# Long convolution: each way-back bank is scaled and emptied by ScalarE into one of four places, with VectorE mixing from there; in the odd layer, both tiles' means stand ahead of one weight quarter

## The chip, the cores and the metric

The kernel runs on one core of a Trainium2 chip. The metric is the device time of one execution in microseconds (us), the median of the runs. Its engines are TensorE (PE, with PEld for its weight loads), VectorE (DVE), ScalarE (ACT), GpSimd (POOL) and SyncE (SP, which issues the weight DMAs). Each engine works through its own instructions in order and waits on semaphores where another engine must have finished first.

## The reference

A latent sequence of 256 tokens and a context of 256 tokens, 1024 wide, in fp32, go through an even layer (a long convolution beside attention), an odd layer (a chunkwise mLSTM), and then two layers of a second model. The two places that the change touches compute this:

```python
def bidir_long_conv(u, filt):
    n = u.shape[1]
    uf = jnp.fft.rfft(u.astype(jnp.float32), n=2 * n, axis=1)
    ff = jnp.fft.rfft(filt, axis=0)
    return jnp.fft.irfft(uf * ff[None], n=2 * n, axis=1)[:, :n].astype(u.dtype)

def hyena_mixer(xv, conv_w, conv_b, f_w1, f_b1, f_freq, f_w2, f_b2, f_w3, hy_bias):
    ...
    x0, x1, v = _split(dw_conv(xv, conv_w, conv_b), (HY_WIDTH, HY_WIDTH, HY_WIDTH))
    filt = hyena_filter(n, f_w1, f_b1, f_freq, f_w2, f_b2, f_w3)
    g = v * x1
    return x0 * (bidir_long_conv(g, filt) + g * hy_bias.astype(g.dtype))
...
        x_lat = x_lat + ga_l[:, None] * rms_norm(y_lat, g_post[layer])
```

The filter is divided by the sum of its absolute values per channel; the kernel applies that factor (`snorm`) to the convolution's result.

## The kernel before

Every fp32 product is made of three fp32r matmuls (lead x lead, lead x rest, rest x lead, line 153). The weights come as a stream: SP loads pieces of 1 MB into a ring of four; ACT rounds each quarter piece to its lead (line 307) and DVE takes the rest (line 144), three quarters ahead of PE; each of the two waits on the one before it. Layers are `Stage` objects whose per-engine programs yield a position in time; `merge` sorts the steps of one engine by that position, and this fixes each engine's order when the program is built. Nothing moves while it runs.

**The long convolution** (`LongConv`) runs between matmul groups of the projections (`dense1`): 2 sequences x 2 halves of 512 channels = 4 rounds. One round: PE transforms tokens to spectra (line 1466), in two halves h = 0 and 1, into PSUM banks 4, 6 and 5, 7 in pairs; ACT copies one bank of each pair (line 1476) and DVE forms sum and difference (lines 1487, 1488); DVE makes twelve products (line 1500) and four folds (line 1526); PE goes back to tokens in four blocks of 128 channels, ch = 0 to 3 (line 1541, 8 short matmuls in the trace). All four blocks write the same half of the same bank, `banks[2]`. After each block DVE runs three steps (`mixes`): it takes the bank times `snorm` into the one scratch `y1` (line 1554, tile `cond`), adds g x bias (line 1556) and multiplies with x0 (line 1557), which raises `lc_mixed`. PE's next block waits for `lc_mixed`, and so do both halves of the next round's spectra. Between two blocks PE has six matmuls of a projection group, in round 1 also four transposes (line 1442), and none between blocks 2 and 3 of round 3, nor between block 3 and the spectra in round 2. The projection groups of that time are the third short convolution (DVE lines 1385 and 1387 after ACT line 1867) and then the gate (ACT line 1896, Silu, and DVE line 1902, which waits for `lc_mixed` of its chunk). PE may write a group's bank again only when DVE has read the group four before it. Line 1585 rounds the sources of the output projection to their leads on ACT.

**The odd layer's seam**: the output projection ends tile 0's two groups first; twelve matmuls of tile 1 follow. `Residual` (tag `or_`) then does for each of two token tiles: ACT squares the two banks with a sum (line 1620), DVE takes the mean (line 1634), ACT the root (line 1628), DVE the reciprocal (line 1642), and DVE twice a product of 512 columns (line 1649) and an addition to x (line 1664). PE's transposes of x for the next layer (line 614, eight blocks) wait for x: the first four blocks for the third addition, the others for the fourth. ACT's leads (line 622) and DVE's rests (line 630) follow each block; blocks 4 to 7 reuse four banks and wait for the rest of the block four before. Where in the queues the steps stand is set by `places`, a row for each tile: position of the squares, of the root (the mean 0.05 ahead of it), of the products, of the additions. `at` is the end of the output projection.

Of the kernel before, what the change touches and what calls it, by code (L numbers as in the profile page):

```python
# [7 lines left out]
ALU = mybir.AluOpType  # L8
ACT = mybir.ActivationFunctionType
# [7 lines left out]
SEQ = 256  # L17
# [1373 lines left out]
class LongConv(Stage):  # L1391
# [4 lines left out]
    def __init__(self, core, room, att, dense, gT, x0T, X, gtok, Y, T2, snorm, banks, start, step):  # L1396
        self.core, self.room, self.att, self.dense, self.gT, self.x0T, self.X = core, room, att, dense, gT, x0T, X
        self.gtok, self.Y, self.T2, self.snorm, self.banks, self.start, self.step = gtok, Y, T2, snorm, banks, start, step
        s = lambda n: core.sem("lc_" + n)
        self.turned, self.tok_ready, self.tabs_turned, self.tabs_ready = s("turned"), s("tok_ready"), s("tabs_turned"), s("tabs_ready")  # L1400
        self.spect, self.copied, self.read, self.made, self.folded = s("spect"), s("copied"), s("read"), s("made"), s("folded")
        self.back, self.mixed = s("back"), s("mixed")
        self.rounds = [(s, j) for s in range(2) for j in range(2)]
        self.tensor, self.vector, self.scalar = (
            (self.tables, self.turns, self.spectra, self.inverse), (self.sums, self.products, self.folds, self.mixes), (self.tables_back, self.tokens, self.copies))

# [46 lines left out]
    def spectra(self, pe):  # L1453
        nc, ps = self.core.nc, self.core.ps
        for r, (s, j) in enumerate(self.rounds):
            for h in range(2):
# [5 lines left out]
                if r:  # L1462
                    pe.wait_ge(self.read, 2 * (r - 1) + h + 1)
                    pe.wait_ge(self.mixed, 4 * r)
                for e in range(2):
# [62 lines left out]
    def inverse(self, pe):  # L1528
        nc, ps = self.core.nc, self.core.ps
        for r, (s, j) in enumerate(self.rounds):  # L1530
            for ch in range(4):
# [5 lines left out]
                if 4 * r + ch:  # L1537
                    pe.wait_ge(self.mixed, 4 * r + ch)
                for e in range(2):
# [3 lines left out]
                mm.then_inc(self.back, 1)  # L1543

    def mixes(self, dve):
        core, nc, link = self.core, self.core.nc, self.core.dve_chain
        for r, (s, j) in enumerate(self.rounds):
            for ch in range(4):
                yield self.at(r) + 5.55 + 0.45 * ch
                k, ss = 4 * j + ch, slice(s * SEQ, (s + 1) * SEQ)  # L1550
                dve.wait_ge(self.back, 4 * r + ch + 1)
                dve.wait_ge(self.dense.dve_read, 2 * KC + k + 1)
                y = self.room.y1
                link(dve, nc.vector.tensor_scalar(y.rearrange("p (m e) -> p m e", e=2), core.ps[:, self.banks[2], 0:SEQ].rearrange("p (e m) -> p m e", e=2),
                                                  self.snorm[:, k:k + 1], None, ALU.mult))
                link(dve, nc.vector.scalar_tensor_tensor(out=y, in0=self.gT[:, k, ss], scalar=core.col("hy_bias", k), in1=y, op0=ALU.mult, op1=ALU.add))
                nc.vector.tensor_tensor(self.x0T[:, k, ss], y, self.x0T[:, k, ss], ALU.mult).then_inc(self.mixed, 1)
# [780 lines left out]
def odd_layer(core, odd):  # L2338
# [46 lines left out]
    def turn_ready(pe, n):  # L2385
        pe.wait_ge(norm.scaled, 2 * n + 2)
        if n < 4:
# [11 lines left out]
                   [core.hT[:, 2 + 2 * i:4 + 2 * i, :].rearrange("p k t -> p (k t)") for i in range(2)],  # L2399
                   [(at - 0.95, at - 0.78, at - 0.74, at - 0.73), (at + 0.01, at + 0.06, at + 0.07, at + 0.08)], parts=2)  # L2400
    end = OddEnd([gates, dense, Program(scalar=(taps,)), heads, norm, turn, out, res], (dense, out), heads, res, at)
# [890 lines left out]
```

## Time and profile before

| | us |
|---|---|
| median of 3 runs | 1885.04 (1884.64 to 1889.12) |
| profiled execution: its time | 1883.9 |
| profiled execution: span, first to last instruction | 1882.1 |
| PE busy | 1808.0 |
| DVE busy | 1141.3 |
| ACT busy | 897.6 |
| mean granted TensorE clock | 0.988 |

PE is busy for 96% of the span, so a microsecond of the kernel's time is either a matmul or one of the few gaps in which PE waits. The waits by releaser name the engine and line that ended each gap. In a timeline the bracket behind a row is the idle time just before it and what ended it; matmuls overlap, so a row's duration is longer than the distance to the next row, and ends are modelled.

### The profile page before, as it was taken

The page shows a single profiled execution, that of the slowest core. Times are in us where ns is not written, and L with a number is a line of the kernel's source. Part 1 is how long each engine was busy: PE and PEld are TensorE (multiplying, and loading weights), DVE is VectorE, ACT ScalarE, POOL GpSimd, SP SyncE. Part 2 cuts the span into 40 slices and gives each one's busy share as a digit, 9 for nine tenths or more (in the row PEclk, how much of TensorE's full clock was granted, in tenths as well). Part 3 has the DMA queues.
Part 4 walks back from the last instruction along what each step waited for, and adds up shares of the span by engine and source line. Part 5 has one row for each costly group of instructions (what it writes and reads, how often), then busy time and mean ns, then how long its engine had stood idle before and what let it go on. Part 6 is the DMA issues. An engine that isn't in the chain of part 4 may idle for free. (4 is left out here: it accounts for less than half of the span.)

```text
span 1882.1 us, 24159 instructions
## 1 busy us (share of the span) xinstructions
PE 1808.0 (96%) x9264; PEld 1474.6 (78%) x9264; DVE 1141.3 (61%) x2038; ACT 897.6 (48%) x1405; POOL 57.1 (3%) x58
## 2 busy tenths in 40 slices
PE   9999999989998999999989999999999999989998
PEld 4777788767787867777778788789987888779986
DVE  5463366687438456666766675666546656566644
ACT  3323444422226346665645556356534646536643
POOL 0000000000000000000100010000000001000000
PEclk9999999999999999999989999999999999999999
DMA  9445311211335324333345444445554444455552
GB/s 342 164 157 201 112 48 65 67 50 63 134 101 180 111 71 139 118 91 116 121 138 168 128 131 156 168 164 183 180 200 154 135 146 136 164 170 168 189 194 88
DMA packets 114843, 264.08 MB, mean 140 GB/s; under 512 B 5111, under 2 KB 9496, under 8 KB 114536
## 3 DMA queue, kind: packets, MB, share of 16 engines
q1 hardware_dynamic: 111528, 252.52, 40.9%
q0 software_dynamic: 2368, 7.70, 1.2%
q10 hardware_dynamic: 832, 2.30, 0.3%
q8 instruction: 74, 1.21, 0.3%
q14 instruction: 41, 0.34, 0.1%
HBM read 261.46 MB, written 1.05 MB: 139 GB/s over the span
## 5 line engine op out<-in xcount | busy, mean ns | idle before, releaser
L144 DVE TENSOR_TENSOR qw_rest<-weights,qw_lead 128x1024 fp32r<-128x1024 f32 (+2 forms) x428 | 522.3, 1223 | 451.8 <-ACT qw_lead L307 450.2
L307 ACT ACTIVATE qw_lead<-weights 128x1024 fp32r<-128x1024 f32 (+2 forms) x428 | 448.3, 1048 | 542.9 <-PE psum L153 529.0
L153 PE MATMUL psum<-qw_lead,b_h_lead 128*128 128x512 f32 (+1 forms) x480 | 198.8, 414 | 9.1 <-DVE hT L3004 5.4
L153 PE MATMUL psum<-qw_lead,b_h_rest 128*128 128x512 f32 (+1 forms) x480 | 188.4, 392 | 0.0
L153 PE MATMUL psum<-qw_rest,b_h_lead 128*128 128x512 f32 (+1 forms) x480 | 187.9, 392 | 0.0
L153 PE MATMUL psum<-b_h_lead,qw_lead 128*128 128x256 f32 x512 | 145.5, 284 | 0.0
L153 PE MATMUL psum<-b_h_rest,qw_lead 128*128 128x256 f32 x512 | 145.2, 284 | 0.0
L153 PE MATMUL psum<-b_h_lead,qw_rest 128*128 128x256 f32 x512 | 145.2, 284 | 0.0
L153 PE MATMUL psum<-e_h_lead,qw_lead 128*128 128x512 f32 x320 | 141.8, 443 | 1.8 <-DVE e_qT L1387 1.4
L153 PE MATMUL psum<-e_h_lead,qw_rest 128*128 128x512 f32 x320 | 126.5, 395 | 0.0
L153 PE MATMUL psum<-e_h_rest,qw_lead 128*128 128x512 f32 x320 | 125.6, 392 | 0.0
L153 PEld LDWEIGHTS psum<-qw_lead,b_h_lead 128*128 128x128 f32 x480 | 91.5, 191 | 30.5 <-DVE hT L3004 6.3
L153 PE MATMUL psum<-qw_lead,o_h_lead 128*128 128x512 f32 x256 | 107.3, 419 | 3.5 <-PEq L118 3.1
L153 PEld LDWEIGHTS psum<-qw_lead,b_h_rest 128*128 128x128 f32 x480 | 91.1, 190 | 19.0
L153 PEld LDWEIGHTS psum<-qw_rest,b_h_lead 128*128 128x128 f32 x480 | 91.6, 191 | 15.2
L153 PE MATMUL psum<-qw_lead,o_h_rest 128*128 128x512 f32 x256 | 100.9, 394 | 0.0
L153 PE MATMUL psum<-qw_rest,o_h_lead 128*128 128x512 f32 x256 | 100.6, 393 | 0.0
L153 PE MATMUL psum<-qw_rest,b_upT_lead 128*128 128x512 f32 x256 | 99.8, 390 | 0.0
L153 PE MATMUL psum<-qw_lead,b_upT_lead 128*128 128x512 f32 x256 | 99.8, 390 | 0.0
L153 PE MATMUL psum<-qw_lead,b_upT_rest 128*128 128x512 f32 x256 | 99.7, 390 | 0.0
L153 PEld LDWEIGHTS psum<-b_h_lead,qw_lead 128*128 128x128 f32 x512 | 98.4, 192 | 0.3
L153 PEld LDWEIGHTS psum<-b_h_rest,qw_lead 128*128 128x128 f32 x512 | 98.4, 192 | 0.0
(480 smaller groups left out, 3482.9 us busy)
## 6 DMA issues: line engine op xcount, KB each, us to landing
weights<-in_w_in SPq DMA_DIRECT2D x48, 1024.0 KB, 5.1
weights<-in_o_w_in SPq DMA_DIRECT2D x32, 1024.0 KB, 5.4
weights<-in_w_mlp_up SPq DMA_DIRECT2D x32, 1024.0 KB, 5.5
weights<-in_w_mlp_down SPq DMA_DIRECT2D x32, 1024.0 KB, 4.8
weights<-in_e_w_in SPq DMA_DIRECT2D x26, 1024.0 KB, 5.2
weights<-in_w_mod SPq DMA_DIRECT2D x24, 1024.0 KB, 7.3
weights<-in_e_w_out SPq DMA_DIRECT2D x8, 1024.0 KB, 4.8
weights<-in_o_w_out SPq DMA_DIRECT2D x8, 1024.0 KB, 4.9
```

The source lines that it names most:

```text
L144: return eng.tensor_tensor(self.rest[at], src, self.lead[at].bitcast(F32), ALU.subtract)
L153: mm = nc.tensor.matmul(out, l, r, start=start and i == 0, stop=stop and i == 2)
L307: self.core.nc.scalar.activation(self.buf.lead[self.at(u)], self.raw(u), ACT.Copy).then_inc(self.lead_ready, 1)
```

## The change

In `LongConv` a new ACT step, `scales`, takes each block out of its bank, times `snorm`, into one of four places (`tokens_of`: two halves of `T2`, `y1`, and half of `Y[3]`, all free in that part of a round) and raises the new semaphore `lc_scaled`. `mixes` on DVE loses its first step and waits for `lc_scaled`; its position goes from 5.55 to 5.70. PE's blocks wait for `lc_scaled` in place of `lc_mixed`, the spectra's second half as well, and the first half for neither. In the odd layer `places` is changed for both tiles. PE's order of instructions is the same as before; the names of its waits differ.

```diff
-        self.back, self.mixed = s("back"), s("mixed")
+        self.back, self.scaled, self.mixed = s("back"), s("scaled"), s("mixed")
...
                 if r:
                     pe.wait_ge(self.read, 2 * (r - 1) + h + 1)
-                    pe.wait_ge(self.mixed, 4 * r)
+                    if h:
+                        pe.wait_ge(self.scaled, 4 * r)
...
                 if 4 * r + ch:
-                    pe.wait_ge(self.mixed, 4 * r + ch)
+                    pe.wait_ge(self.scaled, 4 * r + ch)
...
+    def tokens_of(self, ch):
+
+        return (self.T2[:, 0:SEQ], self.T2[:, SEQ:2 * SEQ], self.room.y1, self.Y[:, 3, 0:SEQ])[ch]
+
+    def scales(self, act):
+        for r in range(len(self.rounds)):
+            for ch in range(4):
+                yield self.at(r) + 5.5 + 0.45 * ch
+                act.wait_ge(self.back, 4 * r + ch + 1)
+                k = 4 * self.rounds[r][1] + ch
+                src = self.core.ps[:, self.banks[2], 0:SEQ].rearrange("p (e m) -> p m e", e=2)
+                self.core.nc.scalar.activation(self.tokens_of(ch).rearrange("p (m e) -> p m e", e=2), src, ACT.Identity,
+                                               scale=self.snorm[:, k:k + 1]).then_inc(self.scaled, 1)
...
-                yield self.at(r) + 5.55 + 0.45 * ch
+                yield self.at(r) + 5.7 + 0.45 * ch
                 k, ss = 4 * j + ch, slice(s * SEQ, (s + 1) * SEQ)
-                dve.wait_ge(self.back, 4 * r + ch + 1)
+                dve.wait_ge(self.scaled, 4 * r + ch + 1)
                 dve.wait_ge(self.dense.dve_read, 2 * KC + k + 1)
-                y = self.room.y1
-                link(dve, nc.vector.tensor_scalar(y.rearrange("p (m e) -> p m e", e=2), core.ps[:, self.banks[2], 0:SEQ].rearrange("p (e m) -> p m e", e=2),
-                                                  self.snorm[:, k:k + 1], None, ALU.mult))
+                y = self.tokens_of(ch)
...
-                   [(at - 0.95, at - 0.78, at - 0.74, at - 0.73), (at + 0.01, at + 0.06, at + 0.07, at + 0.08)], parts=2)
+                   [(at - 1.0, at - 0.99, at - 0.9, at - 0.89), (at - 0.75, at - 0.74, at - 0.78, at - 0.77)], parts=2)
```

VectorE's queue in round 0 of the convolution, around the mix of block 0, before (line 1385 and 1387 finish a group of the short convolution, line 144 a weight quarter, lines 1554 to 1557 are a mix):

```order
L1385 SCALAR_TENSOR_TENSOR e_qT<-psum,cols,e_qT 128x2x255 [waits e_xg_act_read,chunk_done]
L1387 SCALAR_TENSOR_TENSOR e_qT<-psum,cols,e_qT 128x2x255 [waits dve_step]
L1554 TENSOR_SCALAR cond<-psum,small 128x256 [waits e_xg_dve_read,lc_back]
L1556 SCALAR_TENSOR_TENSOR cond<-e_qk,cols,cond 128x256 [waits dve_step]
L1557 TENSOR_TENSOR e_qT<-cond,e_qT 128x256 [waits dve_step]
L144 TENSOR_TENSOR qw_rest<-weights,qw_lead 128x1024 [waits quarter_lead_ready]
L1385 SCALAR_TENSOR_TENSOR e_qT<-psum,cols,e_qT 128x2x255 [waits e_xg_act_read,chunk_done]
L1387 SCALAR_TENSOR_TENSOR e_qT<-psum,cols,e_qT 128x2x255 [waits dve_step]
```

And the same stretch in the changed kernel (a mix is lines 1569 and 1570):

```order
L1385 SCALAR_TENSOR_TENSOR e_qT<-psum,cols,e_qT 128x2x255 [waits e_xg_act_read,chunk_done]
L1387 SCALAR_TENSOR_TENSOR e_qT<-psum,cols,e_qT 128x2x255 [waits dve_step]
L144 TENSOR_TENSOR qw_rest<-weights,qw_lead 128x1024 [waits quarter_lead_ready]
L1385 SCALAR_TENSOR_TENSOR e_qT<-psum,cols,e_qT 128x2x255 [waits e_xg_act_read,chunk_done]
L1387 SCALAR_TENSOR_TENSOR e_qT<-psum,cols,e_qT 128x2x255 [waits dve_step]
L1569 SCALAR_TENSOR_TENSOR e_qT<-e_qk,cols,e_qT 128x256 [waits e_xg_dve_read,lc_scaled]
L1570 TENSOR_TENSOR e_qT<-e_qT 128x256 [waits dve_step]
```

The first mix now stands behind the quarter and the last group of the short convolution, and it no longer reads the bank.

ScalarE's queue in round 3 of the changed kernel (line 1557 is the new scale, line 1598 a source's lead, which was line 1585, line 307 a weight quarter's lead, line 1909 the gate's Silu):

```order
L307 ACTIVATE qw_lead<-weights 128x1024 [waits chunk_done,half_landed2]
L1557 ACTIVATE e_qT<-psum,small 128x256 [waits lc_back] x2
L1557 ACTIVATE cond<-psum,small 128x256 [waits lc_back]
L1598 ACTIVATE e_h_lead<-hT 128x512 [waits chunk_done,ea_out_done]
L307 ACTIVATE qw_lead<-weights 128x1024 [waits chunk_done,half_landed3]
L1557 ACTIVATE x_res<-psum,small 128x256 [waits lc_back]
L1909 ACTIVATE e_qT<-psum 128x512 [waits e_xg_dve_read,chunk_done] x3
```

Without the four scales the rows are those of before; the last scale stands behind a source's lead and a weight quarter's lead.

VectorE's queue at the odd layer's seam, before, from the first product of tile 0 on:

```order
L1649 SCALAR_TENSOR_TENSOR hT<-psum,small,ga 128x512 [waits dve_step]
L1664 TENSOR_TENSOR x_res<-x_res,hT 128x512 [waits or_read]
L1649 SCALAR_TENSOR_TENSOR hT<-psum,small,ga 128x512
L1664 TENSOR_TENSOR x_res<-x_res,hT 128x512 [waits or_read]
L144 TENSOR_TENSOR qw_rest<-weights,qw_lead 128x1024 [waits quarter_lead_ready]
L1634 TENSOR_SCALAR small<-small 128x1 [waits or_squared]
L1642 RECIPROCAL small<-small 128x1 [waits or_rooted]
L1649 SCALAR_TENSOR_TENSOR hT<-psum,small,ga 128x512 [waits dve_step]
```

And in the changed kernel, from the same step on to the first rests of the next layer:

```order
L1662 SCALAR_TENSOR_TENSOR hT<-psum,small,ga 128x512 [waits dve_step]
L1677 TENSOR_TENSOR x_res<-x_res,hT 128x512 [waits or_read]
L1662 SCALAR_TENSOR_TENSOR hT<-psum,small,ga 128x512
L1677 TENSOR_TENSOR x_res<-x_res,hT 128x512 [waits or_read]
L1647 TENSOR_SCALAR small<-small 128x1 [waits or_squared]
L1655 RECIPROCAL small<-small 128x1 [waits or_rooted]
L1662 SCALAR_TENSOR_TENSOR hT<-psum,small,ga 128x512 [waits dve_step]
L1677 TENSOR_TENSOR x_res<-x_res,hT 128x512 [waits or_read]
L1662 SCALAR_TENSOR_TENSOR hT<-psum,small,ga 128x512
L1677 TENSOR_TENSOR x_res<-x_res,hT 128x512 [waits or_read]
L144 TENSOR_TENSOR qw_rest<-weights,qw_lead 128x1024 [waits quarter_lead_ready]
L630 SCALAR_TENSOR_TENSOR b_h_rest<-psum,cols,b_h_lead 128x256 [waits b0_n1_lead_out] x8
```

The quarter went from between the tiles to behind tile 1. On ScalarE tile 0's squares and root (lines 1620 and 1628) went from behind a weight quarter's lead to ahead of it; tile 1's squares now follow that lead.

## Rows read from the trace of the kernel before

**Rows 1.** Waits of PE by releaser: us in total, times, longest.
```profile
PE psum L1541 <- DVE e_qT L1557: 7.1, 10, 2.5
PE psum L614 <- DVE x_res L1664: 6.2, 1, 6.2
...
PE psum L1466 <- DVE e_qT L1557: 3.6, 3, 1.7
```
**Rows 2.** Timeline of PE, round 0: start, us, what, idle before.
```profile
378.24 0.47 PE L153 MATMUL psum<-e_h_lead,qw_lead 128*128 128x512 f32 x1 [1.45 <-DVE e_qT L1387]
...
382.40 0.71 PE L1541 MATMUL psum<-hy_dft,hy_F 128*128 128x128 f32 x4 [2.53 <-DVE e_qT L1557]
...
389.08 0.71 PE L1541 MATMUL psum<-hy_dft,hy_F 128*128 128x128 f32 x4 [0.17 <-DVE e_qT L1557]
389.63 0.61 PE L1541 MATMUL psum<-hy_dft,e_qk 128*128 128x128 f32 x4
389.99 0.47 PE L153 MATMUL psum<-e_h_lead,qw_lead 128*128 128x512 f32 x1
...
391.89 1.96 PE L1466 MATMUL psum<-x_res,hy_dft 128*128 128x512 f32 x4 [0.26 <-DVE e_qT L1557]
```
**Rows 3.** Timeline of PE, round 1.
```profile
409.56 0.63 PE L1442 MATMUL psum<-ident,e_qk 128*128 128x128 f32 x4
410.03 0.66 PE L1541 MATMUL psum<-hy_dft,hy_F 128*128 128x128 f32 x4
...
415.04 0.48 PE L153 MATMUL psum<-e_h_lead,qw_lead 128*128 128x512 f32 x1
...
416.52 0.63 PE L1442 MATMUL psum<-ident,e_qk 128*128 128x128 f32 x4
...
424.40 3.67 PE L1466 MATMUL psum<-x_res,hy_dft 128*128 128x512 f32 x8 [1.68 <-DVE e_qT L1557]
```
**Rows 4.** Timeline of PE, rounds 2 and 3.
```profile
441.55 0.61 PE L1541 MATMUL psum<-hy_dft,hy_F 128*128 128x128 f32 x4
...
452.40 1.96 PE L1466 MATMUL psum<-x_res,hy_dft 128*128 128x512 f32 x4 [1.65 <-DVE e_qT L1557]
...
472.10 0.71 PE L1541 MATMUL psum<-hy_dft,hy_F 128*128 128x128 f32 x4 [0.98 <-DVE e_qk L1526]
...
480.64 0.71 PE L1541 MATMUL psum<-hy_dft,hy_F 128*128 128x128 f32 x4 [1.55 <-DVE e_qT L1557]
```
**Rows 5.** Busy by stretch: us, PE, PEld, DVE, ACT, POOL, clock, DMA share, GB/s.
```profile
382.00:392.00 10.00, 9.17 (x43) 7.06 (x44) 6.98 (x13) 0.00 (x0) 0.00 (x0) 0.83 0.32 107
```
**Rows 6.** By line, ScalarE's and VectorE's: duration ns min/median/max, first and last start.
```profile
L1842 ACT ACTIVATE e_qT<-psum,small x5: 466/468/470, 117.9 to 170.6; 128x256 f32<-128x256 f32 x5
...
L1554 DVE TENSOR_SCALAR cond<-psum,small x16: 475/484/486, 380.9 to 482.2; 128x256 f32<-128x256 f32 x16
```
**Rows 7.** Timeline of ScalarE ahead of the first Silu of round 2.
```profile
442.88 1.28 ACT L1896 ACT_TABLE_LOAD   x1
```
**Rows 8.** Timeline of ScalarE at the odd layer's seam.
```profile
968.87 1.06 ACT L307 ACTIVATE qw_lead<-weights 128x1024 fp32r<-128x1024 f32 x1 [3.02 <-PE psum L153]
969.84 1.01 ACT L1620 ACTIVATE hT<-psum 128x1024 f32<-128x1024 f32 x1
```
**Rows 9.** Timeline of VectorE at the odd layer's seam.
```profile
974.37 1.22 DVE L144 TENSOR_TENSOR qw_rest<-weights,qw_lead 128x1024 fp32r<-128x1024 f32 x1
975.51 0.14 DVE L1634 TENSOR_SCALAR small<-small 128x1 f32<-128x1 f32 x1
...
978.91 3.59 DVE L630 SCALAR_TENSOR_TENSOR b_h_rest<-psum,cols,b_h_lead 128x256 fp32r<-128x256 f32 x8
```
**Rows 10.** Timeline of PE at the odd layer's seam.
```profile
967.02 0.39 PE L153 MATMUL psum<-qw_lead,o_hsT_rest 128*128 128x512 f32 x1
...
977.65 3.81 PE L614 MATMUL psum<-ident,x_res 128*128 128x128 f32 x16 [6.21 <-DVE x_res L1664]
981.12 0.78 PE L153 MATMUL psum<-qw_lead,b_h_lead 128*128 128x512 f32 x1
```

More of the change, by code:

```diff
@@ L1401, in __init__ @@
         self.spect, self.copied, self.read, self.made, self.folded = s("spect"), s("copied"), s("read"), s("made"), s("folded")
-        self.back, self.mixed = s("back"), s("mixed")
+        self.back, self.scaled, self.mixed = s("back"), s("scaled"), s("mixed")
         self.rounds = [(s, j) for s in range(2) for j in range(2)]
         self.tensor, self.vector, self.scalar = (
-            (self.tables, self.turns, self.spectra, self.inverse), (self.sums, self.products, self.folds, self.mixes), (self.tables_back, self.tokens, self.copies))
+            (self.tables, self.turns, self.spectra, self.inverse), (self.sums, self.products, self.folds, self.mixes), (self.tables_back, self.tokens, self.copies, self.scales))
     def at(self, r):
```

## The prediction

> **What bounds the kernel now.** I began with the busy shares: PE is busy for 1808 of 1882 us, so only PE's gaps can be won. The second view is therefore PE's waits by releaser [rows 1]. Two of its releasers are touched by the change. The mix's last step on VectorE (line 1557) ends 10 gaps ahead of the way-back blocks and 3 ahead of the spectra, together 10.7 us; the last step of the odd layer's residual (line 1664) ends one gap of 6.2 us. The third view is PE's timeline in the four rounds [rows 2 to 4] and at the seam [rows 10], where the reader is to see not the bracketed gaps alone but the distance from one point that does not depend on them to the next. That distance also holds what a gap costs around itself: matmuls are pipelined, so every stop adds about 0.16 us of refill (389.99 to 391.89 is 1.90 us: 0.26 of gap, 1.48 for the group by the pace below, and 0.16 [rows 2]), and in round 0 the granted clock fell. It was 0.83 on the mean over 382 to 392 us [rows 5]: of its two levels, 1.2 and 2.4 GHz, PE had the lower one for a good third of that time, right after the stop of 2.53 us [rows 2].
>
> **PE's pace without waits.** A way-back block takes 0.91 us of PE to the next instruction (389.08 to 389.99), and its last matmul ends 1.16 us after its start (389.63 + 0.61) [rows 2]. A group of six projection matmuls takes 1.48 us (415.04 to 416.52), four transposes 0.47 us (409.56 to 410.03) [rows 3]. A block and a group are 2.39 us.
>
> **The scale on ScalarE.** Sixteen new ACT instructions. The nearest row is line 1842, the same size from PSUM with a scale from a tile: 0.47 us [rows 6]. The new one reads two halves in turn; no row shows that on ScalarE. On VectorE line 1554 has just this pattern and takes 0.48 us [rows 6], which is why I take 0.47 and not the far end, the 1.01 us of a row of four times the elements from PSUM [rows 8]. Below 0.47 nothing is won, since PE does not wait for it, as follows. The scale starts 0.04 us after the block's end and PE restarts 0.06 us after it, so the bank is free 1.16 + 0.04 + 0.47 + 0.06 = 1.73 us after the block began, and PE comes back at 2.39. Slack: 0.66 us, so a scale of up to 1.13 us is free, and even the far end of 1.01 costs PE nothing there (only block 3 of round 3 would be 0.54 later). In round 0 ScalarE has nothing else queued in this stretch. Elsewhere a scale can stand behind one short-convolution output or one weight lead; by ScalarE's order each of these is ready before the block ends, but for the last scale of round 3.
> The Trainium skill speaks against the move: "ScalarE: Activation LUTs", section "Rules for kernel authors", would leave multiplications to VectorE as the faster engine per element. The rows do not bear this out at this size: 0.47 us on ScalarE against the 0.48 of the step replaced. By the page's cost formula (fixed part plus 0.83 ns per element) a scale would be an estimated 0.49 us, and the sum would be the same within 0.02.
>
> **VectorE.** It loses 16 first steps, and the mix that remains no longer holds the bank. What is late next there: PE's groups wait until VectorE has read the group four before (line 1387), and the sums of the next round. In round 0 the first mix stood ahead of a weight quarter and of the fourth group's read; now it stands behind both, so that this read moves from behind mix and quarter (1.37 + 1.22 us) to behind the quarter alone, earlier than now, while the four mixes (0.86 us each without their first step) end near 387.0 and the next sums are due at 389.5. Both are covered. The wait of 1.45 us at 378.24 [rows 2] stays: its queue is unchanged.
>
> **Round 0.** From 378.24 PE runs a group, then three times block and group, to the spectra: 378.24 + 1.48 + 3 x 2.39 = 386.89, where they stand at 391.89 now. Gain 5.00: 2.96 of gaps, some 1.5 of low clock, the rest refill. For the clock both ends are kept: if it falls all the same, 1.5 less.
> **Round 1.** From block 0 at 410.03: 4 x 2.39 + 2 x 0.47 = 10.50, so the spectra stand at 420.53 and not at 424.40 [rows 3]. Gain 3.87.
> **Round 2.** From 441.55: 3 x 2.39 + 0.91 gives 449.63 against 452.40 [rows 4]. Gain 2.77. Here ScalarE changes to Silu between two scales. The load takes 1.28 us [rows 7] and hits between blocks 1 and 2, after the scale that block 2 needs; it delays a Silu, and VectorE's gate step, for which PE has no need in this round.
> **Round 3.** Block 0 at 472.10 waits for VectorE's folds [rows 4]; the change takes nothing out of that chain. Block 2 starts at 472.10 + 4.78 = 476.88; block 3 follows with nothing between them: bank free at 476.88 + 1.73 = 478.61, where it is 480.64 now. Gain 2.03, and 0.6 us of wait stays. The last scale then stands behind a source's lead and a weight lead, which delays the last mix by about 1 us, but no PE instruction waits for that bank again and the gate steps behind it are set by PE's quarter and come as early as block 3. So the gain is kept up to the output projection.
> Sum of the convolution: 5.00 + 3.87 + 2.77 + 2.03 = 13.67 us. Between rounds the chains from spectra to folds move as a whole. Weight leads are shifted by up to 2 us in rounds 2 and 3; a quarter is prepared three quarters ahead, and 24 matmuls of PE stand in each, so this costs nothing.
>
> **The seam.** Tile 0's groups are complete after the matmul at 967.02 [rows 10], at 967.41, but its squares start at 969.84, behind a weight lead that waits for PE until 968.87 [rows 8]. Ahead of it, the squares start 2.4 us earlier, and so does VectorE's work on tile 0, which ends at 971.98 and not 974.37 [rows 9]. Tile 1's last matmul ends twelve later, near 970.14; its squares, 1.0 us and the accumulator, are done near 971.3. So tile 1's mean runs at 971.98 instead of 975.51: 2.39 from tile 0, 1.14 from the quarter that stood between. That quarter is not gone: it now stands between tile 1 and the rests. The third addition, for which PE's transposes wait, moves from 977.6 to 974.1, 3.5 us; the rests, 3.40 us behind the mean, would move as much, but pay the 1.14: 976.52 in place of 978.91. PE's first projection matmul, 2.21 us behind the first rest (981.12 against 978.91 [rows 9, 10]), follows the rests, since blocks 4 to 7 wait for their banks. Gain 2.39, not the 6.2 of the waits. For the bounds: PE still stops for some 2.7 us, like the 2.53 us after which the clock fell in round 0, so I leave the low clock here as it is (the first matmul at 0.78 us); if it stays up, at most 1.3 us more. If something I do not see holds tile 1, nothing is gained.
>
> **Sum.** 13.67 + 2.39 = 16.06 us. The profiled execution took 1883.9 us, so 1867.8; the median of the runs is 1.1 above that execution, so **1868.9 us**.
>
> **Rivals.**
> Forecast: both parts as worked out, 1866.5 to 1871.5. Chance 0.62.
> *Only the waits go.* In round 0 PE's clock falls anyway (1.5 less), and at the seam rests and leads in a new order give nothing (2.4 less): 1872.8. For it: PE's stop of 1.45 us ahead of the long one stays. Against: right after it, at 378.24, the matmul took 0.47 us, as at 389.99 at the full clock [rows 2]. Chance 0.20.
> *More than the sum.* The clock at the seam stays up, and the waits on VectorE shrink elsewhere, since it has 16 x 0.48 = 7.7 us less to do: 1866. Chance 0.07.
> *ScalarE must change tables for each scale.* If it did, a scale would take 1.28 + 0.47 = 1.75 us [rows 6, 7], 0.62 over the slack of 1.13, with refill 0.8 at each of some 11 gates: 8.6 less won, 1877.5. The order of the changed kernel holds no load more than before, against it. The Trainium skill, same page, section on table sets, says that identity is in every set, which is the same result. Chance 0.04.
> *The scale is slow: slower than before.* Place: the 12 gates from block to block and to the spectra, ScalarE reading two interleaved halves of a bank and writing every second element. Each costs PE the scale's time above 1.13 us. The whole gain is gone at 1.13 + 16.1/12 = 2.5 us a scale, and from 3.0 us on the kernel is slower by over 0.3%: 1891 and up. For it: no row of ScalarE has this pattern. Against: VectorE's 0.48 with the same pattern. Chance 0.07: 0.04 within 0.3%, 0.03 beyond.
> That the change doesn't do what it says would need PE to wait for the mix after all; the changed order shows `lc_mixed` on PE only at the output projection. I give it nothing of its own.
>
> **How the numbers follow.** 0.3% of 1885, 5.7 us, is about what a measurement can tell from no change. Faster: 0.62 + 0.20 + 0.07 + 0.04 = 0.93, then 0.04 for the same and 0.03 for slower. The range takes in the forecast, the case of waits alone and the larger gain, with some 2 us for what a seam or a run may add: 1865 to 1875.5; it leaves out the last two.
>
> **What would show it.** In the profile of the changed kernel no wait of PE should be released by the mix; ScalarE's new line should read near 470 ns; the clock should stay 1.00 in the stretch of round 0; one gap of about 0.6 us before the last block of round 3; at the seam a gap of about 2.7 us, then transposes held by the rests. DVE's busy time should fall by 7.7 us and ACT's rise by 7.5. It is wrong if scales read over 1.1 us, if VectorE's reads (line 1387) or a weight quarter end new gaps in the rounds, or if the projection after the seam starts as late behind the last output matmul as before.

## The result, and the profile after

The changed kernel takes 1869.2 us (median of 4 runs, 1867.9 to 1869.6) beside 1885.4 us for the kernel before; the ratio is 0.9909, interval 0.9892 to 0.9926. The prediction was 1868.9. In a later comparison the same kernel gave 1865.4 us and 0.9895 (0.9879 to 0.9912); the experiments show where such a difference comes from. The profiled execution has a span of 1867.8 us where before it was 1882.1.

Busy times of the changed kernel (the page's first part), then the waits of PE by releaser that answer to [rows 1]: us in total, times, longest.

```profile
PE 1805.2 (97%) x9264; PEld 1474.6 (79%) x9264; DVE 1134.2 (61%) x2022; ACT 904.4 (48%) x1421; POOL 57.0 (3%) x58
```
```profile
PE psum L614 <- DVE b_h_rest L630: 3.8, 4, 1.9
...
PE psum L614 <- DVE x_res L1677: 2.7, 1, 2.7
...
PE psum L1542 <- ACT cond L1557: 0.6, 1, 0.6
```

(The convolution's and the residual's lines stand 1 to 13 further down than before: the block is line 1542, the spectra 1467, the scale 1557, the residual's last step 1677.) No gap is released by the mix any more: of its 10.7 us, 0.6 is left under the new scale's name. The seam's one gap of 6.2 is now 2.7 and 1.9. DVE fell by 7.1 us, ACT rose by 6.8.

PE's timeline of round 0, against [rows 2], and the clock in the stretch that answers to [rows 5] (us, PE busy, clock, DMA share, GB/s):

```profile
379.73 0.47 PE L153 MATMUL psum<-e_h_lead,qw_lead 128*128 128x512 f32 x1 [1.45 <-DVE e_qT L1387]
...
381.18 0.60 PE L1542 MATMUL psum<-hy_dft,hy_F 128*128 128x128 f32 x4
...
381.99 0.48 PE L153 MATMUL psum<-e_h_lead,qw_lead 128*128 128x512 f32 x1
...
383.45 0.60 PE L1542 MATMUL psum<-hy_dft,hy_F 128*128 128x128 f32 x4
...
385.72 0.60 PE L1542 MATMUL psum<-hy_dft,hy_F 128*128 128x128 f32 x4
...
387.98 1.88 PE L1467 MATMUL psum<-x_res,hy_dft 128*128 128x512 f32 x4
```
```profile
381.00:391.00 10.00, 10.00 (x54) 1.00 0.33 107
```

ScalarE's scale of the block at 381.18:

```profile
382.27 0.48 ACT L1557 ACTIVATE e_qT<-psum,small 128x256 f32<-128x256 f32 x1 [3.48 <-PE psum L1542]
```

Three blocks (1 to 3 of the round) follow each other every 2.27 us with no bracket between, and the clock is 1.00 where it was 0.83. Of the 2.27 the block takes 0.81 (381.18 to 381.99) and the group 1.46 (381.99 to 383.45). The other rounds, against [rows 3, 4], down to the first matmul of the output projection:

```profile
406.07 0.64 PE L1542 MATMUL psum<-hy_dft,hy_F 128*128 128x128 f32 x4
...
416.15 3.59 PE L1467 MATMUL psum<-x_res,hy_dft 128*128 128x512 f32 x8
...
433.19 0.60 PE L1542 MATMUL psum<-hy_dft,hy_F 128*128 128x128 f32 x4
...
440.88 1.88 PE L1467 MATMUL psum<-x_res,hy_dft 128*128 128x512 f32 x4
...
460.51 0.71 PE L1542 MATMUL psum<-hy_dft,hy_F 128*128 128x128 f32 x4 [1.00 <-DVE e_qk L1527]
...
462.90 0.60 PE L1542 MATMUL psum<-hy_dft,hy_F 128*128 128x128 f32 x4
...
466.78 0.71 PE L1542 MATMUL psum<-hy_dft,hy_F 128*128 128x128 f32 x4 [0.56 <-ACT cond L1557]
...
476.57 0.47 PE L153 MATMUL psum<-qw_lead,e_h_lead 128*128 128x512 f32 x1 [1.13 <-DVE e_qT L1915]
```

The output projection's row stood in the kernel before at:

```profile
490.45 0.47 PE L153 MATMUL psum<-qw_lead,e_h_lead 128*128 128x512 f32 x1 [1.13 <-DVE e_qT L1902]
```

So I measure the convolution by one distance, from the group behind block 0 of round 0 to that row: 490.45 - 378.24 = 112.21 before, 476.57 - 379.73 = 96.84 after, 15.37 us less. The seam, against [rows 8 to 10], PE and then VectorE:

```profile
955.75 1.47 PE L690 MATMUL psum<-ident,ga 128*128 128x128 f32 x12
959.92 1.09 PE L614 MATMUL psum<-ident,x_res 128*128 128x128 f32 x8 [2.71 <-DVE x_res L1677]
962.93 1.94 PE L614 MATMUL psum<-ident,x_res 128*128 128x128 f32 x8 [1.91 <-DVE b_h_rest L630]
964.52 0.77 PE L153 MATMUL psum<-qw_lead,b_h_lead 128*128 128x512 f32 x1
...
968.08 0.63 PE L153 MATMUL psum<-qw_lead,b_h_rest 128*128 128x512 f32 x1
968.51 0.55 PE L153 MATMUL psum<-qw_lead,b_h_lead 128*128 128x512 f32 x1
968.89 0.39 PE L153 MATMUL psum<-qw_rest,b_h_lead 128*128 128x512 f32 x1
```
```profile
961.18 1.22 DVE L144 TENSOR_TENSOR qw_rest<-weights,qw_lead 128x1024 fp32r<-128x1024 f32 x1
962.31 1.65 DVE L630 SCALAR_TENSOR_TENSOR b_h_rest<-psum,cols,b_h_lead 128x256 fp32r<-128x256 f32 x4
```

From the twelve transposes of `ga` (line 690), which wait for nothing here, to the first projection matmul it is 8.77 us; before it was 981.12 - 969.98 = 11.14. But ten projection matmuls then run at the lower clock (0.77, 0.63 and 0.55 us instead of 0.39), where before there were six (a row of 0.39 us is one at the full clock).

**The account.** The same points in both traces show where 14.3 us of span came from (us; "won" is the time before minus the time after, and the last column what the stretch added):

| point | before | after | won | in the stretch |
|---|---|---|---|---|
| first wait for a quarter's rest | 53.67 | 53.51 | 0.16 | 0.16 |
| group behind block 0, round 0 | 378.24 | 379.73 | -1.49 | -1.65 |
| output projection of the even layer | 490.45 | 476.57 | 13.88 | **15.37** |
| transposes of `ga` | 969.98 | 955.75 | 14.23 | 0.35 |
| gates of the next layer (line 2548, was 2535) | 1053.59 | 1037.79 | 15.80 | **1.57** |
| transposes of line 614, one layer part on | 1243.86 | 1226.57 | 17.29 | 1.49 |
| transposes of line 690, next layer | 1511.84 | 1495.81 | 16.03 | -1.26 |
| branches of that layer | 1629.71 | 1615.32 | 14.39 | -1.64 |
| transposes of line 614 | 1692.23 | 1676.55 | 15.68 | 1.29 |
| end | 1882.1 | 1867.8 | 14.3 | -1.38 |

The two parts of the change gave 16.94 us; the other stretches gave and took up to 1.65 us at a time, together -2.6. No wait differs there by over 0.5 us; what does is the granted clock. From 50 to 100 us it was 0.93 before and 0.90 after, 50 x 0.03 = 1.5 us:

```profile
50.00:100.00 50.00, 47.65 (x225) 0.90 0.38 132
```

### The profile page after: what moved, and what is told of

It reads as the page before. It is cut to its first block and busy times, and to the rows that moved or that the text cites. A ratio compares the mean times of both kernels' runs of the same rounds, so it can differ in the third digit from the quotient of the medians.

```text
span 1867.8 us, 24160 instructions
## 1 busy us (share of the span) xinstructions
PE 1805.2 (97%) x9264; PEld 1474.6 (79%) x9264; DVE 1134.2 (61%) x2022; ACT 904.4 (48%) x1421; POOL 57.0 (3%) x58
## 5 line engine op out<-in xcount | busy, mean ns | idle before, releaser
L153 PEld LDWEIGHTS psum<-b_h_lead,qw_rest 128*128 128x128 f32 x512 | 98.8, 193 | 0.0
```

The lines of the kernel that those rows point to most:

```text
L153: mm = nc.tensor.matmul(out, l, r, start=start and i == 0, stop=stop and i == 2)
```

## Experiments

Each kernel below is the changed kernel with one edit, if nothing else is said. "Distance" is the one defined above (96.84), "seam" the one from the transposes of `ga` to the first projection matmul (8.77).

### The two parts alone

```diff
-                   [(at - 1.0, at - 0.99, at - 0.9, at - 0.89), (at - 0.75, at - 0.74, at - 0.78, at - 0.77)], parts=2)
+                   [(at - 0.95, at - 0.78, at - 0.74, at - 0.73), (at + 0.01, at + 0.06, at + 0.07, at + 0.08)], parts=2)
```

> The convolution's part alone; the odd layer's `places` are those of before. Theory (the two parts add up, and the convolution gave 15.4 us of the distance from the first projection matmul behind block 0 of round 0 to the output projection, 112.2 before and 96.8 in the changed kernel): that distance reads 96.8 +- 0.3, the seam reads as before (11.1 us from the twelve transposes of `ga` to the first projection matmul), and the time is near 1870.0 us, 0.8 to 2 us above the changed kernel. Rival (the seam's part gives nothing, only a wait is renamed): the same time as the changed kernel, 1869.2, within 0.3.

Measured: distance 474.70 - 377.84 = 96.86, seam 11.15 with its one gap of 6.21; 1870.3 us, ratio 0.9914 (0.9901 to 0.9928). The convolution's part alone carries nearly all. Its ratio's interval overlaps that of the changed kernel, so run times can't tell the theory from the rival here; the trace does.

The other way round, the kernel before with the new `places` only:

> The odd layer's `places` alone; the convolution is that of before. Theory: from the twelve transposes of `ga` to the first projection matmul 8.8 us instead of 11.1, but ten projection matmuls at the lower clock (0.43 us apart) instead of five or six, so about 1.6 us and not 2.4 are won: near 1883.8 us. First rival (the prediction's term, the low clock left as it is): 2.4, 1883.0. Second rival (nothing): 1885.4. The convolution's distance stays at 112.2.

Measured: distance 112.18, seam 8.78; 1885.0 us, ratio 0.9989 (0.9980 to 0.9998), which is 0.95 us under the 1885.95 of the kernel before beside it, where 1.6 was expected. PE at the seam of this kernel, and the clock there:

```profile
974.32 1.09 PE L614 MATMUL psum<-ident,x_res 128*128 128x128 f32 x8 [2.70 <-DVE x_res L1664]
977.33 1.94 PE L614 MATMUL psum<-ident,x_res 128*128 128x128 f32 x8 [1.92 <-DVE b_h_rest L630]
978.92 0.78 PE L153 MATMUL psum<-qw_lead,b_h_lead 128*128 128x512 f32 x1
979.49 0.63 PE L153 MATMUL psum<-qw_rest,b_h_lead 128*128 128x512 f32 x1
979.92 0.60 PE L153 MATMUL psum<-qw_lead,b_h_rest 128*128 128x512 f32 x1
980.35 0.40 PE L153 MATMUL psum<-qw_lead,b_h_lead 128*128 128x512 f32 x1
```

The waits are those of the changed kernel to 0.02 us, yet three matmuls run slow and not ten. Up to the gates of the next layer, which takes the slow matmuls in, the stretch from `ga` reads 83.61 and 83.34 us with the old places (before, and the kernel above), and with the new ones either 80.69 to 80.88 (this kernel and three below) or 81.97 to 82.05 (the changed kernel and three more). So the new places gain about 1.5 or about 2.7 us by the trace, by where the clock comes back up; the expected count of ten slow matmuls was a reading of one execution. What decides between the two outcomes is not shown: both traces of the changed kernel (the second stands below) have the longer one.

### What empties the bank, and into what

Four places, but VectorE takes the bank:

```diff
-                self.core.nc.scalar.activation(self.tokens_of(ch).rearrange("p (m e) -> p m e", e=2), src, ACT.Identity,
-                                               scale=self.snorm[:, k:k + 1]).then_inc(self.scaled, 1)
+                self.core.nc.vector.tensor_scalar(self.tokens_of(ch).rearrange("p (m e) -> p m e", e=2), src, self.snorm[:, k:k + 1],
+                                                  None, ALU.mult).then_inc(self.scaled, 1)
```

> Four places as in the changed kernel, but VectorE takes the bank, in the place in its queue of the first step of the old mix; the mix stays at its new place. This tells the move to ScalarE from the four places. Theory (what counts is that the bank is released after one step; which engine does it matters only where VectorE's queue is full): in round 0 the take of block 1 stands behind a quarter, a group's two steps and the mix of block 0, about 1.0 us late, and in round 1 VectorE has 2.84 us of work for each 2.72 us of PE, so 1 to 2 us there: the distance from behind block 0 of round 0 to the output projection reads 98.5 to 100.5, the time is 1871 to 1873. Rival (ScalarE is the point: a bank taken by VectorE waits in its queue as before): the distance reads 105 or more, the time 1877 or more.

Measured: distance 480.18 - 378.60 = 101.58, 1873.2 us, ratio 0.9928 (0.9915 to 0.9942). PE in round 0:

```profile
381.78 0.71 PE L1542 MATMUL psum<-hy_dft,hy_F 128*128 128x128 f32 x4 [1.56 <-DVE e_qT L1557]
...
385.61 0.71 PE L1542 MATMUL psum<-hy_dft,hy_F 128*128 128x128 f32 x4 [1.28 <-DVE e_qT L1557]
```

4.7 us of the 15.4 are lost, more than the theory's 1.7 to 3.7 and less than the rival's 8: 3.4 of it in round 0 (378.60 to the spectra at 390.26, 11.66 against 8.25), 0.8 in round 1, 0.5 at the output projection. Freeing the bank after one step is worth two thirds whoever does it; the last third comes from an engine whose queue is empty there. I was low in round 0 because I had misread which block the rows are: the block at 381.18 is block 1, and its bank is released by the take of block 0, which on VectorE stands behind three groups' steps.

ScalarE takes the bank, but always into `y1`, so each scale waits for the mix before it:

```diff
-        return (self.T2[:, 0:SEQ], self.T2[:, SEQ:2 * SEQ], self.room.y1, self.Y[:, 3, 0:SEQ])[ch]
+        return self.room.y1
...
                 act.wait_ge(self.back, 4 * r + ch + 1)
+                if 4 * r + ch:
+                    act.wait_ge(self.mixed, 4 * r + ch)
```

> ScalarE takes the bank, but into one place (`y1`) for all blocks, so each scale also waits for the mix of the block before. This tells what the other three places give. Theory: in the changed kernel the mix of a block ends before the next scale starts everywhere but in round 0, where the first mixes stand behind a quarter: mix 0 ends at 385.9 there and scale 1 starts at 384.5, so round 0 grows by 1.0 to 1.5 us and no other; distance 98.0 to 98.4, time near 1870.4. Rival (the places are the point, since PE again waits for a mix at second hand): half of the gain or more is gone, distance 104 or more, time 1877 or more.

Measured: distance 101.63 and 1870.2 us, ratio 0.9916 (0.9903 to 0.9930). PE in round 0, and two stretches with the clock:

```profile
388.03 0.71 PE L1542 MATMUL psum<-hy_dft,hy_F 128*128 128x128 f32 x4 [2.89 <-ACT cond L1559]
...
394.28 1.88 PE L1467 MATMUL psum<-x_res,hy_dft 128*128 128x512 f32 x4
```
```profile
382.00:392.00 10.00, 7.11 (x36) 0.87 0.32 107
392.00:402.00 10.00, 10.00 (x39) 0.96 0.00 0
```

The theory is right that only round 0 changes, and wrong by a factor of three on its size, by the same misreading: in the changed kernel scale 1 is the one at 382.27 and not the one at 384.5, that is 2.5 us behind the group's start at 379.73, and here it waits for mix 0 and starts 6.3 us behind the group (387.50 against 381.25). Round 0 takes 13.03 us, nearly the 13.65 of before. One stop of 2.89 us costs 3.05 (refill with it), and behind it the clock falls (0.87 and 0.96, together 1.7 us). So the four places are worth 4.8 us in this trace, all in round 0, where the first mix stands behind a weight quarter and the fourth group's steps. The run times show only 1 us of it, inside their spread. Not run were two or three places, and one place with the mixes at their old position 5.55, ahead of that quarter: so it is open how much of the 4.8 us is the price of the mixes' new position.

### How much slack a scale has

A second, spare scale ahead of each real one (`c` is the chain semaphore of ScalarE):

```diff
+                self.core.nc.scalar.activation(self.Y[:, 0, 0:SEQ].rearrange("p (m e) -> p m e", e=2), src, ACT.Identity, scale=self.snorm[:, k:k + 1]).then_inc(c.sem, 1)
...
```

> The changed kernel with a second, spare scale ahead of each real one (same source, an unused place as its target), so that a bank is held for two scales, 0.94 us instead of 0.47. The prediction says that up to 1.13 us are free; the changed kernel's own pace of 2.27 us from block to block makes that 2.27 - 1.16 - 0.04 - 0.06 = 1.01 us. Theory: only the last block of round 3, which follows the one ahead of it with nothing between, moves by 0.47; the distance from behind block 0 of round 0 to the output projection goes from 96.84 to 97.3, the time to about 1869.7 us. Rival (there is no slack; PE's return is set by the scale at each block): 0.47 at each of 13 gates, distance 102 to 103, time near 1875.

Measured: distance 97.45, 1868.9 us, ratio 0.9905 (0.9889 to 0.9922). The one gap of PE that grew, and ScalarE's two instructions behind the first gated block of round 0:

```profile
467.48 0.71 PE L1543 MATMUL psum<-hy_dft,hy_F 128*128 128x128 f32 x4 [0.93 <-ACT cond L1563]
```

```profile
382.36 0.47 ACT L1561 ACTIVATE x_res<-psum,small 128x256 f32<-128x256 f32 x1 [3.12 <-PE psum L1543]
382.74 0.47 ACT L1563 ACTIVATE e_qT<-psum,small 128x256 f32<-128x256 f32 x1
```

0.56 became 0.93; no gate between blocks appeared. The two scales overlap: the second starts 0.38 us behind the first, so the bank was held for 382.74 + 0.47 - 382.36 = 0.85 us and not for 0.94, and the last block of round 3 lost 0.37 and not 0.47. The remaining 0.25 us of the distance came ahead of round 3's first block. Then two spare instructions, of 1024 and of 512 columns, ahead of each:

```diff
+                self.core.nc.scalar.activation(self.Y[:, 0:2, :], self.Y[:, 0:2, :], ACT.Identity).then_inc(c.sem, 1)
+                self.core.nc.scalar.activation(self.Y[:, 2, :], self.Y[:, 2, :], ACT.Identity).then_inc(c.sem, 1)
...
```

> The changed kernel with two spare ScalarE instructions of 1024 and 512 columns ahead of each scale, so that a bank is held for about 1.9 us. Theory (threshold 1.01 us): the bank is free 3.2 us after a block's start where PE comes back at 2.27, so eight gates (two in round 0, one in round 1, three in round 2, two in round 3) lose 1.05 each, two gates of round 1 with transposes between lose 0.6 each, the last block of round 3 1.4: 11 us, and up to 3 more where ScalarE's own queue (short convolution, Silu with its table) is held up or the clock falls at a stop. Distance 107.5 to 111, time 1880 to 1884. Rival (the prediction's count of 12 gates with a threshold of 1.13): 12 x 0.9 + 1.4 = 12, the same sum but with gaps ahead of the spectra too, which the theory has not.

Measured: distance 488.56 - 379.71 = 108.85, 1881.4 us, ratio 0.9971 (0.9958 to 0.9984). Three of its gates, and ScalarE behind the block at 381.18:

```profile
384.26 0.71 PE L1543 MATMUL psum<-hy_dft,hy_F 128*128 128x128 f32 x4 [0.66 <-ACT e_qT L1564]
387.45 0.71 PE L1543 MATMUL psum<-hy_dft,hy_F 128*128 128x128 f32 x4 [0.64 <-ACT cond L1564]
...
477.29 1.22 PE L1543 MATMUL psum<-hy_dft,hy_F 128*128 128x128 f32 x4 [2.03 <-ACT cond L1564]
```

```profile
382.27 1.06 ACT L1561 ACTIVATE x_res<-x_res 128x1024 f32<-128x1024 f32 x1 [2.04 <-PE psum L1543]
...
383.76 0.45 ACT L1564 ACTIVATE e_qT<-psum,small 128x256 f32<-128x256 f32 x1
```

The bank was held from 382.27 to 384.21, 1.94 us. The block at 381.18 follows no stop: ScalarE starts 1.09 us behind its start, PE restarts 0.05 us after ScalarE's end, and without a wait PE would be back after 2.27. That leaves 2.27 - 1.09 - 0.05 = 1.13 us of slack, and the next block came 1.94 - 1.13 = 0.81 us late (384.26 instead of 383.45). From then on each block follows a stop and takes 0.92 us instead of 0.81 (384.26 to 385.18), and from gate to gate it is 3.19 us, 0.92 more than 2.27. So the slack is the prediction's 1.13 and not the 1.01 of my expectations, which had taken the end of a block behind a stop (1.16) together with the pace of one without (2.27); no run lies between 0.85 us held, which costs nothing there, and 1.94. The mechanism works at ten gates and the last block. No gap stands ahead of any spectra, since their first half no longer waits. Part of the 12.0 us is clock: behind the stop of 2.03 it was 0.67 over 475 to 480 us, and from there to the output projection it is 11.27 us instead of 9.79. That last point was tried by itself:

```diff
-                    if h:
-                        pe.wait_ge(self.scaled, 4 * r)
+                    pe.wait_ge(self.scaled, 4 * r)
```

> The changed kernel with the wait for `lc_scaled` put back on the first half of each round's spectra too. Theory (the bank is free 1.73 us after a block's start): ahead of the spectra of rounds 1 and 2, where a projection group stands between, nothing; ahead of those of round 3, which follow block 3 of round 2 directly, a gap of about 0.7 and with refill 0.85 us: distance 97.7, time 0.9 above the changed kernel. Rival (the two halves of the spectra do not need the bank so early, ScalarE is just ahead everywhere): nothing at all, 96.8.

Measured: distance 97.76 and exactly one new gap, where block 3 of round 2 is followed directly by the spectra; 1867.7 us, ratio 0.9907 (0.9892 to 0.9921).

```profile
439.97 1.96 PE L1466 MATMUL psum<-x_res,hy_dft 128*128 128x512 f32 x4 [0.66 <-ACT x_res L1556]
```

The dropped wait is worth 0.9 us, in one round.

### The seam: the quarter and the clock

The weight quarter behind the eight rests instead of ahead of them:

```diff
+        late = self.core.stream.split_no[self.core.stream.first["o_out"] + 15] + 3
         for i, at in self.ahead():
-            yield at + self.offsets[1]
+            yield at + self.offsets[1] + (3.4 if i == late else 0)
```

> The changed kernel, with the weight quarter's rest that stands between tile 1's last addition and the rests of the next layer put behind the eight rests. This measures the prediction's term of 1.14 us for the quarter. Theory: the rests start 1.1 us earlier, PE's second stop at the seam shrinks from 1.91 us to 0.8, the first projection matmul stands 7.6 us after the transposes of `ga` instead of 8.8; nothing else waits for that quarter, which PE needs 8 us later. Time 1.1 us less than the changed kernel, near 1868. Rival (rests are bound by ScalarE's leads and by the four banks, not by VectorE's queue): 8.8 stays. Second rival: the quarter comes late, and PE gets a new wait on `qw_rest` in the first projection of the next layer, or the load behind it does, which gives the 1.1 back.

Measured: seam 963.01 - 955.46 = 7.55, the second stop 0.78, no new wait; 1868.2 us, ratio 0.9903 (0.9887 to 0.9918). Its four runs go from 1864.1 to 1871.4, so the median can't show 1.1 us.

```profile
961.51 1.84 PE L615 MATMUL psum<-ident,x_res 128*128 128x128 f32 x8 [0.78 <-DVE b_h_rest L631]
963.01 0.78 PE L153 MATMUL psum<-qw_lead,b_h_lead 128*128 128x512 f32 x1
```

The quarter's term, 1.14 in the prediction, measures 1.13 in the stop (0.78 instead of 1.91); the rest of the 1.22 is that the transposes behind it take 1.50 us and not 1.59. Next, TensorE kept at work in both stops:

```diff
+    def keep_busy(pe):
+        yield odd_end.at + 0.25
+        odd_end.turn_free(pe)
+        for i in range(18):
+            nc.tensor.transpose(ps[:, 5, 0:P], core.ident[:], core.ident[:])
+        yield t0 - 2.5 + 0.85
+        for i in range(12):
+            nc.tensor.transpose(ps[:, 0, 0:P], core.ident[:], core.ident[:])
```

> The changed kernel with 30 spare transposes of the identity on TensorE in the two stops of the seam (18 ahead of the third addition's wait, 12 between the two halves of the transposes), into banks that are free there. They compute nothing that is used. Theory (the clock falls there because PE stands still): the granted clock stays 1.00 across the seam, no projection matmul behind it is 0.43 us apart, so the 24th of them stands 14.0 us after the transposes of `ga`; in the four profiles with these places so far it stood at 16.1, 14.8, 14.9 and 14.8. Time 1 to 2 us less than the changed kernel, 1867.2 to 1868.2. The first projection matmul stays at 8.8, since the rests on VectorE set it. Rival (the low clock is not a matter of standing still): low stretch stays, 24th at 14.8 or more, time as the changed kernel or, if the spare transposes run into the real ones, later.

Measured: the clock is 1.00 from 955 to 970 us and no projection matmul is slow; seam 8.46, since the transposes themselves run at the full clock; 1866.1 us, ratio 0.9894 (0.9879 to 0.9909). Up to the gates of the next layer the stretch from `ga` is 79.70 us where it was 80.7 or 82.0.

```profile
958.22 1.09 PE L614 MATMUL psum<-ident,x_res 128*128 128x128 f32 x8 [0.74 <-DVE x_res L1677]
959.14 1.47 PE L2783 MATMUL psum<-ident 128*128 128x128 f32 x12
961.23 1.52 PE L614 MATMUL psum<-ident,x_res 128*128 128x128 f32 x8 [0.61 <-DVE b_h_rest L630]
962.50 0.48 PE L153 MATMUL psum<-qw_lead,b_h_lead 128*128 128x512 f32 x1
```

In the eleven traces of these experiments in which the stops are not filled (the old places, the new ones, the shorter second stop) the clock falls at the seam; with the stops filled it does not, here and in the next run. So the low clock at the seam comes from standing still. And both together, with 5 spare transposes in the second stop:

> The changed kernel with both edits that helped one by one: the weight quarter's rest behind the eight rests, and spare transposes in the two stops (18 ahead of the third addition's wait, 5 between the halves; they compute nothing that is used). Theory (the two add up: one shortens the second stop by 1.1 us, the other keeps the clock up across the seam): first projection matmul 7.3 us after the transposes of `ga` (8.77 in the changed kernel, 7.55 and 8.46 with one edit each), the clock 1.00 from there on, time 1865 us, 4 less than the changed kernel. Rival (they share one gain, since a shorter stop already spares the clock): not under the kernel with spare transposes alone, 1866.1.

Measured: seam 962.80 - 955.47 = 7.33, clock 1.00 there, 78.62 us up to the gates of the next layer; 1865.2 us (1859.7 to 1865.8), ratio 0.9886 (0.9871 to 0.9900). At the first projection matmul the two edits add up: 1.44 us, with 1.22 and 0.31 for each alone. Up to the gates they read 79.79 and 79.70 us alone and 78.62 together. Against the 82.0 of the changed kernel that is 2.3 and 2.3 alone but 3.4 together, so part of the gain is shared, as the rival has it; against the other outcome of these places, about 80.8, it is 1.0, 1.1 and 2.2, and they add up. These traces can't tell which of the two comparisons is the right one.

### The same program twice

> The changed kernel once more, unchanged, beside the others on the same chip. It tells what one profile of the same program differs from another by. Theory (TensorE's low clock comes in portions, each costs PE about 1.7 us, and their number and place vary between executions of the same program while all waits stay the same): the convolution's distance reads 96.8 and the first projection matmul of the seam 8.77 again, within 0.05, but the portions stand in part elsewhere, and run times spread over 3 us or more together with the mean clock. Rival: the portions are where they were, and what differs between kernels' sums is due to their edits.

Measured: distance 96.87, seam 8.78 with the same two stops, and 81.97 up to the gates: all as in the first profile to 0.1 us. The median was 1865.4 us (1864.9 to 1866.7), 3.8 under the first; within this comparison the four runs spread over only 1.9 us and not over the expected 3. It stood beside the kernel with both seam edits on the same chip and took the same time, although the seam is 3.4 us shorter there. The stretch from 50 to 80 us, untouched by either, accounts for that in the profiled pair (this kernel's row first, then that of the kernel with both edits):

```profile
50.00:80.00 30.00, 27.65 (x151) 0.94 0.52 182
```
```profile
50.00:80.00 30.00, 27.66 (x136) 0.83 0.43 153
```

30 x 0.11 = 3.3 us; the group behind block 0 of round 0 stands at 376.54 in one and at 379.79 in the other. The rival falls: portions of low clock come and go in the same code. Whole executions show it too: the 15 runs of the kernel before that stood beside the first four experiments go from 1881.6 us at a mean clock of 0.990 to 1889.0 at 0.984. So that both seam edits beat the changed kernel is shown at their place, and not by the medians.

## Why the prediction was right, point by point

- **Total.** 1868.9 predicted, 1869.2 measured. By the profiled pair the parts gave 15.37 + 1.57 = 16.94 where 16.06 were expected, and untouched stretches took back 2.6 of clock. So the profiled executions differ by 14.3, and the medians by 16.2 only because the profiled execution of before was 1.1 us below the median then known and that of after 0.4 above its own. That the forecast came within 0.3 us is luck, as the same kernel's 1865.4 shows; that too is inside the range.
- **Pace.** The one term sized wrongly in every round: block and group take 2.27 us and not 2.39. The block's 0.91 was read from one behind a stop of 0.17 us [rows 2]; a block that follows no stop takes 0.81, and the group to the next block 1.46 instead of 1.48. Behind a stop the prediction's pace holds to 0.01: block 0 of round 3, which waits for the folds, has the next one 2.39 us behind it (460.51 to 462.90). So removing a stop gave 0.10 us more than gap and refill, which the sum had left out. That is 0.40 more won in round 0, 0.42 in round 1, 0.39 in round 2 and 0.24 in round 3: gains of 5.40, 4.29, 3.16 and 2.27 where 5.00, 3.87, 2.77 and 2.03 were predicted. The remaining 0.25 lies between the rounds.
- **Scale.** 474 to 476 ns in the trace (medians of three groups), 0.47 predicted. The Trainium skill, "ScalarE: Activation LUTs", section "Rules for kernel authors", would leave multiplications to VectorE, with a figure for bf16; for this fp32 step the trace does not bear that out: 475 ns against VectorE's 484 [rows 6], and with VectorE doing it the distance is 4.7 us longer.
- **Slack.** The mechanism was right. The 1.13 us came out as well, but by two errors that cancel: pace and end of the block were both taken with the 0.1 us that a block takes longer behind a stop. The gates are ten and the last block instead of 12. A bank held for 0.85 us cost 0.6 us in all, one held for 1.94 us cost 12.0.
- **VectorE.** No wait took the mix's place. But the prediction passed over what the places do in round 0: it named the mixes that end near 387.0 as covered, and did not say that with a single place that very lateness would hold PE for 2.9 us.
- **Clock in round 0.** It stayed at 1.00, as the forecast case has it and the first rival has not. With stops of 1.56 and 1.28 us it stayed up too; behind 2.89, and behind 2.03 in the run with a bank held for 1.94 us, it fell again.
- **Round 3.** The last block waits 0.56 us (0.6 predicted), and from it to the output projection it is 9.79 us where it was 9.81: the last mix is late for nobody.
- **Seam.** 11.14 - 8.77 = 2.37 for 2.39 predicted, gaps 2.71 and then rests, as named. "I leave the low clock here as it is" is the step that failed in the profiled execution: there are ten slow matmuls instead of six, 0.8 us of the 2.37. Other kernels with the same places had three or four. It was no constant to be left, but a quantity with two outcomes, 1.3 us apart. As the waits of the seam were right, this is a size and not the mechanism. The Trainium skill, "TensorE: Matmul & The Clock Gate", section "What's actually happening", says that the count of slow matmuls at a kernel's start varies from run to run of one kernel. The changed kernel's two traces agree away from the start, with a clock of 0.83 and 0.94 over 50 to 80 us; at the seam itself both have ten slow matmuls.

## What to carry to other kernels

A bank that gates TensorE should be emptied in one step by the engine with the shortest queue at that point, into as many places as the later steps can lag; the lag, not the step's duration, decides how many. Whether two places would have done was not run. Price a removed wait by the distance between two points that it doesn't touch, and take the pace from instructions that follow no stop. When two profiles are compared, walk down points common to both, since untouched stretches can differ by more than the edit under test.

## What was not expected of the hardware

- TensorE's low clock shows in portions that cost about 1.7 us each (0.83 over ten busy microseconds: in the changed kernel's first trace at 60, 70, 570, 650, 1410 and 1590 us); their place and number vary between executions of one program with the same waits (at 60 us there is none in its second trace).
- With 30 spare transposes of the identity in the seam's two stops the clock stayed at 1.00, and 79.70 us passed where it had been 80.7 to 82.0. Work that computes nothing was worth 1.0 to 2.3 us at that place.
- At the same stops (2.70 and 1.92 us) the clock came back after three slow matmuls in the kernel with the places alone and after ten in the changed kernel.
- A block of 8 short matmuls takes 0.81 us to the next instruction where nothing stops PE ahead of it, and 0.91 to 0.92 behind a stop of 0.17 us or 0.66 us alike.
